# Half of the last gate chunk computed behind the first query, and first gathers in other places, in a two-layer hybrid encoder with an expert layer

## The chip, the cores and the metric
One core of a Trainium2 chip. The metric is device time in microseconds, lower is better. Everything is float32. TensorE is "PE", VectorE "DVE", ScalarE "ACT", GpSimd "POOL", SyncE "SP" in the profile.

## The reference, cut to what matters
256 tokens of 1024 features go through two layers. In each:

```
h = rmsnorm(x); proj = h @ w_in          # q, k, v, z, xbc, dt, gate_logits (2 x 1024 columns)
a_out = rmsnorm(diff_attention(q, k, v)) @ w_att_br
m_out = rmsnorm(ssd(xbc, dt) * silu(z)) @ w_ssm_br
g_att, g_ssm = split(sigmoid(gate_logits + gate_b))
x = x + (g_att * a_out + g_ssm * m_out) @ w_out
h = rmsnorm(x); qry = h @ wq             # 8 heads x 2 halves x 128
top 16 of 128 keys for both halves, top 16 of the 256 sums, softmax -> gate
x = x + sum_k gelu(u[idx_k] . h) * gate_k * v[idx_k]      # 8 x 16 = 128 experts a token
```

and a final rmsnorm. Each token has its own experts, so u and v rows are fetched by index.

## The kernel before
Tokens lie in two blocks of 128. The kernel is one hand-written program for each engine; they meet by counting semaphores. A layer has two stretches.

**Products.** Weights come through SP's queue in chunks of 128 x 4096 (2 MB) into two ring slots (w_ring), in the order of w_stream; a chunk's load waits for the first product of the chunk before it. hT holds the normed input with features on partitions. `half(c, u, m)` makes two tiles of 128 output features from a chunk, for all 256 tokens: 2 tiles x 8 k-steps, and each float32 matmul shows as two instructions, 32 in all. The last two chunks in front of the SSM branch's output product are the gate chunks C_GSSM and C_GSSM + 1 (the second gives features 512 to 1023 of g_ssm); units ("g", 2) and ("g", 3) stand around the product of the last SSM group (L651). While the last unit runs, VectorE, ScalarE and GpSimd finish the gated y of group 7, its squares and their sum. The sum of squares gives r_bc, the norm's factor. Then L460 makes m_out, 16 k-steps, four chunks; VectorE mixes (L1428 to L1433): gateT = g_att * a_out + r_bc * g_ssm * m_out. `out_product(b, c, ks)` multiplies the mixed rows of block b by half c of w_out; `add_half`/`add_quarter` on VectorE add them to x_tok. Block one's normed x is turned on TensorE (`turn_half`, `turn_quarter`) into hT and its first query (head 0) is made (`query_tiles(0, 0, ...)`), then its scores (`key_scores(0, 0)`), from the PSUM bank of which VectorE picks the first experts (`first_eight`, `other_eight`). Behind it come block two's out products, its turns, and the other queries, some of them (LATE) one tile at a time between pairs.

**Gathers.** A layer has 2 x 128 slots (block, head, rank). A slot is one indirect DMA by GpSimd (L1814): for each of the 128 tokens one row of u and v, 8 KB, 1 MB in all. Two slots are a pair; there are 128 pairs, m = 0 to 127. Five places hold pairs: ring = [a, w, d, f, c], by the lists FIRST_PLACES and PLACES. They lie over other things: w is slot 0 of w_ring (holds the first half of w_out), c lies over wq0 (first query weights), d over out1 (second half of w_out); a and f are free. So GpSimd waits, in its own order, before pair 1 (w) for out_product(1, 0), before pair 2 (d) for out_product(1, 1), before pair 6 (c) for the queries of wq0; and for `pair_used`, the product of the pair that had the place. A pair goes: gather; VectorE `dots(m)`, two multiply-and-sum of 128 x 1024 (L1671); ScalarE `weigh`: gelu (L1083), times gate (L1088), a diagonal matrix (L1095); TensorE L790, diagonals times v rows, onto the x that waits in PSUM; then the place is free. For m < 126 the steps are by pair, for the last two pairs by row.
`route(p)` on VectorE, a generator of 21 steps, makes the experts of PARTS[p] (one or two heads) between the dots: `begun_at` says with which pair it begins, and a fixed number of steps is taken behind each pair's dots. GpSimd waits for `experts_ready` before it goes on to the next part: part 1 is pairs 8 to 15, part 2 pairs 16 to 31.
ScalarE's order at the start of the stretch is written out too: `query_out` and `scores_out` copy what TensorE made, `turned(j)` copies block two's turned x, `gate_exp(p)` makes the softmax's exponentials, and they stand between the `weigh` calls.

**The end of a layer.** Block two's sums are copied out of PSUM (L1684, L839), squared (L829), the root and its reciprocal made, x normed into xn (L1219), turned (L449), copied with the gain into hT (L851), and the first product of the next layer begins; after the last layer the final norm and the store follow.

```
                for i in range(4):
                    dve.wait_ge(mix_full.sem, mix_full.at(L, 4 + i + 1))
                    step(dve.tensor_tensor(s_tmp[:, 0:2, :], two(i), gateT[:, KD + 2 * i:KD + 2 * i + 2, :], ALU.mult))
                    g = gateT[:, 2 * i:2 * i + 2, :]
                    dve.tensor_tensor(g, g, s_tmp[:, 0:2, :], ALU.add).then_inc(mix_empty.sem, 1)
```

## Time and profile before

| | us |
|---|---|
| time, median of 3 runs | 2267.85 (2266.72 to 2267.86) |
| the profiled execution's own time | 2270.27 |
| its span, first to last instruction | 2268.5 |
| TensorE matmul busy | 1770.3 (78%) |
| VectorE busy | 1348.1 (59%) |
| ScalarE busy | 737.3 (33%) |
| GpSimd busy | 600.2 (26%) |
| moved by DMA | 706.57 MB, mean 311 GB/s |

Busy shares are means over the stretches named above, which have different limits. A matmul's busy time is modelled and overlaps the next one's, so durations of runs of matmuls are better read from the chain of waits, where pieces do not overlap. Times of rows count from the start of the span. Layer one is 0 to about 1130, layer two the rest; the first gathers are issued at 478.92 and 1604.62.

### The profile page before, as it was taken

How to read it: one execution, taken by the hardware profiler on the slowest of the kernel's cores; microseconds unless marked ns; L12 is line 12 of the kernel's file. 1: busy time of each engine (PE TensorE's matmuls, PEld its weight loads, DVE VectorE, ACT ScalarE, POOL GpSimd, SP SyncE). 2: the span in 40 equal slices, each digit the busy share in tenths (PEclk: the TensorE clock that was granted, in tenths of full speed). 3: DMA queues.
4: the chain of work that ended last, by engine and by line, in shares of the span. 5: the costliest groups of instructions: out<-in, count | busy, mean ns of one | idle time of the engine just before them, and what ended most of it. 6: DMA issues, size and time to landing. Idle time of an engine off the chain costs nothing.

```text
span 2268.5 us, 26730 instructions
## 1 busy us (share of the span) xinstructions
PE 1770.3 (78%) x10064; PEld 1091.6 (48%) x10064; DVE 1348.1 (59%) x3219; ACT 737.3 (33%) x2055; POOL 600.2 (26%) x598
## 2 busy tenths in 40 slices
PE   8999999997666655555599999999977557555555
PEld 7688888864222211111186888888633222111111
DVE  3377377168776576664424674761686766676644
...
GB/s 200 153 113 148 149 221 152 287 274 421 421 421 421 421 421 421 422 422 420 375 150 119 144 123 185 193 153 284 323 420 421 421 421 421 421 422 421 422 420 294
DMA packets 91474, 706.57 MB, mean 311 GB/s; under 512 B 10800, under 2 KB 10928, under 8 KB 16848
## 3 DMA queue, kind: packets, MB, share of 16 engines
...
q14 instruction: 51, 0.42, 0.0%
...
## 4 chain that ended last, share of the span: by engine, by line
PE 50%; DMA 34%; DVE 8%; ACT 3%; POOL 2%; issue 2%; SPq 0%; POOLq 0%; DVEq 0%; ACTq 0%
PE bank L477 25%; DMA ring_c<-in_peer_uv,ex_i 13%; DMA ring_d<-in_peer_uv,ex_i 11%; DMA w_ring<-in_peer_uv,ex_i 7%; PE bank L790 6%; PE bank L460 5%; DMA ring_a<-in_peer_uv,ex_i 3%; PE bank L609 2%; PE bank L498 2%; DVE ring_c L1671 2%; PE bank L671 2%; PE bank L724 2%; DVE ring_d L1671 2%; DVE w_ring L1671 1%; ACT diag L1095 1%
## 5 line engine op out<-in xcount | busy, mean ns | idle before, releaser
L477 PE MATMUL bank<-hT,w_ring 128*128 128x256 f32 x2560 | 566.2, 381 | 0.2 <-DMA w_ring<-in_w_stream 0.2
L477 PEld LDWEIGHTS bank<-hT,w_ring 128*128 128x128 f32 x2560 | 484.0, 191 | 71.3 <-issue 6.6
L1083 ACT ACTIVATE gel<-act_u 128x2 f32<-128x2 f32 x260 | 52.8, 203 | 814.7 <-DVE ring_d L1671 173.3
L790 PE MATMUL bank<-ring_a,diag 64*64 64x512 f32 x832 | 137.9, 792 | 97.4 <-ACT diag L1095 97.4
L790 PE MATMUL bank<-ring_d,diag 64*64 64x512 f32 x832 | 134.5, 772 | 98.4 <-ACT diag L1095 98.1
L790 PE MATMUL bank<-w_ring,diag 64*64 64x512 f32 x832 | 135.0, 777 | 96.5 <-ACT diag L1095 96.5
L790 PE MATMUL bank<-ring_f,diag 64*64 64x512 f32 x800 | 131.9, 788 | 93.5 <-ACT diag L1095 93.3
L790 PE MATMUL bank<-ring_c,diag 64*64 64x512 f32 x800 | 128.0, 766 | 90.0 <-ACT diag L1095 90.0
L1814 POOL DMA_INDIRECT ring_a<-in_peer_uv,ex_i x104 | 108.4, 1043 | 306.9 <-DVE ex_i L1591 163.2
L1671 DVE SCALAR_TENSOR_TENSOR ring_a<-ring_a,h 128x1024 f32<-128x1024 f32 x104 | 123.3, 1223 | 87.4 <-DMA ring_a<-in_peer_uv,ex_i 87.2
L1671 DVE SCALAR_TENSOR_TENSOR ring_d<-ring_d,h 128x1024 f32<-128x1024 f32 x104 | 123.5, 1224 | 85.6 <-DMA ring_d<-in_peer_uv,ex_i 85.4
L1671 DVE SCALAR_TENSOR_TENSOR w_ring<-w_ring,h 128x1024 f32<-128x1024 f32 x104 | 123.3, 1222 | 81.0 <-DMA w_ring<-in_peer_uv,ex_i 80.9
L1671 DVE SCALAR_TENSOR_TENSOR ring_c<-ring_c,h 128x1024 f32<-128x1024 f32 x100 | 118.7, 1223 | 83.7 <-DMA ring_c<-in_peer_uv,ex_i 83.3
L1671 DVE SCALAR_TENSOR_TENSOR ring_f<-ring_f,h 128x1024 f32<-128x1024 f32 x100 | 118.6, 1224 | 81.5 <-DMA ring_f<-in_peer_uv,ex_i 81.4
L1095 ACT ACTIVATE diag<-cst,wgt 128x64 f32<-128x64 f32 x512 | 150.6, 340 | 8.5
L1814 POOL DMA_INDIRECT ring_d<-in_peer_uv,ex_i x104 | 110.6, 1063 | 150.5 <-PE bank L790 124.8
L1814 POOL DMA_INDIRECT w_ring<-in_peer_uv,ex_i x104 | 106.7, 1026 | 149.4 <-PE bank L790 132.6
L1814 POOL DMA_INDIRECT ring_c<-in_peer_uv,ex_i x100 | 105.3, 1053 | 148.6 <-PE bank L790 127.7
L1814 POOL DMA_INDIRECT ring_f<-in_peer_uv,ex_i x100 | 103.7, 1037 | 144.5 <-PE bank L790 128.0
L1088 ACT ACTIVATE wgt<-gel,gate_w 128x1 f32<-128x1 f32 x512 | 123.4, 287 | 9.6
L790 PEld LDWEIGHTS bank<-ring_a,diag 64*64 64x64 f32 x832 | 32.9, 163 | 194.3 <-ACT diag L1095 151.2
L790 PEld LDWEIGHTS bank<-w_ring,diag 64*64 64x64 f32 x832 | 32.2, 160 | 187.6 <-ACT diag L1095 145.7
...
## 6 DMA issues: line engine op xcount, KB each, us to landing
w_ring<-in_w_stream SPq DMA_DIRECT2D x60, 2048.0 KB, 8.3
...
wq<-in_w_stream SPq DMA_DIRECT2D x6, 2048.0 KB, 12.7
out<-in_w_stream SPq DMA_DIRECT2D x2, 2048.0 KB, 14.9
...
```

Source lines behind the costliest of these rows:

```text
L460: ins = pe.matmul(two(b0 + j // 2)[:, j % 2, :], w[:, k, j * P:(j + 1) * P], rhs(k), start=(k == 0), stop=(k == ks - 1))
L477: ins = pe.matmul(two(m % 2)[:, j % 2, :], w[:, k, j * P:(j + 1) * P], hT[:, k, :], start=(k == 0), stop=(k == KD - 1))
L498: ins = pe.matmul(bank[m % 2][:], hT[:, k, b * P:(b + 1) * P], w[:, k, :], start=(k == 0), stop=(k == KD - 1))
L609: ins = pe.matmul(two(2 + i % 2)[:, j, :], w[:, k, col:col + P], attT[:, k, :], start=(k == 0), stop=(k == KD - 1))
L671: ins = pe.matmul(bank[4 + 2 * b + c][:], gateT[:, k, b * P:(b + 1) * P], w[:, k, :], start=(k == 0), stop=(k == KD - 1))
L724: ins = pe.matmul(to[:, j * P:(j + 1) * P], w[:, k, col:col + P], hT[:, k, b * P:(b + 1) * P], start=(k == 0), stop=(k == KD - 1))
L790: ins = pe.matmul(bank[b0 + half_of][n * HB:(n + 1) * HB, :], diag[tokens, PAIR * (m % 2) + s, :], ring[PLACE[m]][tokens, s, DM + n * 512: ...
L1083: act.activation(gel[:, b, c0:c1], act_u[:, b, c0:c1], ACT.Gelu).then_inc(gelu_done.sem, 1)
L1088: ins = act.activation(wgt[:, b, j + s:j + s + 1], gel[:, b, j + s:j + s + 1], ACT.Copy, scale=gates[:, j + s:j + s + 1])
L1095: ins = act.activation(diag[:, PAIR * (m % 2) + s, :], const("blocks"), ACT.Copy, scale=wgt[:, b, j + s:j + s + 1])
L1671: ins = dve.scalar_tensor_tensor(out=row, in0=row, scalar=1.0, in1=h2[:, b, :], op0=ALU.mult, op1=ALU.mult, accum_out=act_u[:, b, PAIR * k ...
L1814: pool.indirect_dma_start(ring[q][:, s, :], None, peer_uv, bass.IndirectOffsetOnAxis(ap=ex_i[:, b, j:j + 1], axis=0))\
```

## The change
- **Gate chunk.** C_GSSM + 1 is multiplied with block one's 128 tokens only. A second load of the same chunk, gate_w1 (over ring place a), is issued by SP behind wq0, and `late_gate` makes block two's 4 tiles of 128 x 128 from it, three of its 32 matmuls before the first key scores, the others behind them. ScalarE takes the sigmoid into sc's slot 1. 
- **Mixed rows.** Block one's mixed rows stay in gateT, block two's go to a tensor of their own, mixT. For its features 512 to 1023 VectorE keeps g_att * a_out in mixT and r_bc * m_out in qryT, and `mix_late` puts them together with the late gate; out_product(1, 0) waits for this before k = 4. r_bc lies elsewhere.
- **Order.** query_tiles(2, 0) and turn_half(1, 1) move behind pair 0, and the queries and scores that follow each move one pair later, as do the first LATE tiles, the routes of parts 1 and 2 (begun with pairs 2 and 9) and ScalarE's copies; seven route steps a pair instead of six; gate_exp(0) before turned(0); softmax(0) before dots(0).
- **Places.** The first eight pairs go round f, a, w, d; place c comes in with pair 12. GpSimd waits for the late gate before pair 1, for out_product(1, 0) before pair 2, for out_product(1, 1) before pair 3.
- **Last row.** The last slot of a layer is gathered as two DMAs, its u half and its v half, with indices of their own; the dots wait for the first, TensorE for the second. Its diagonal is made from the gate ahead, and scaled by gelu.
- **Layer change.** Squares of block two, xn and the copies into hT are divided between ScalarE and VectorE; the exponential of alog comes behind them.

```diff
-M_QK, M_V, M_XBC, M_GATT, M_ATT, M_Z, M_GSSM, M_NORM2, FILLS = 4, 12, 16, 32, 36, 40, 48, 52, 75
...
-ROUTE_FILLS = [("t", 0, 0), ("t", 1, 0), ("t", 2, 0), ("q", 0, 0), ("s", 0, 0), ("t", 0, 1), ("q", 2, 0), ("t", 1, 1), ("s", 2, 0),
+M_QK, M_V, M_XBC, M_GATT, M_ATT, M_Z, M_GSSM, M_NORM2, FILLS = 4, 12, 16, 32, 36, 40, 48, 52, 76
...
+ROUTE_FILLS = [("t", 0, 0), ("t", 1, 0), ("t", 2, 0), ("q", 0, 0), ("s", 0, 0), ("g", 0, 1), ("t", 0, 1), ("q", 2, 0), ("t", 1, 1), ("s", 2, 0),
...
-LATE = [(4, 0, (1, 2, 3, 4)), (8, 0, (5, 7, 9, 11)), (12, 0, (15, 17, 19, 21)), (4, 1, (24, 26, 28, 30)),
+LATE = [(4, 0, (3, 4, 5, 6)), (8, 0, (5, 7, 9, 11)), (12, 0, (15, 17, 19, 21)), (4, 1, (24, 26, 28, 30)),
...
-FIRST_PLACES, PLACES = (0, 1, 2, 3), (0, 1, 4, 2, 3)
+FIRST_PLACES, PLACES = (3, 0, 1, 2, 3, 0, 1, 2), (3, 0, 1, 2, 4)
...
-PLACE = [FIRST_PLACES[m] if m < 4 else PLACES[(m - 4) % RING_PAIRS] for m in range(LAYER_PAIRS)]
+ALONE = len(FIRST_PLACES)
+PLACE = [FIRST_PLACES[m] if m < ALONE else PLACES[(m - ALONE) % RING_PAIRS] for m in range(LAYER_PAIRS)]
...
-        pair_a, at = place(at, "ring_a", [P, PAIR, 2 * DM])
+        pair_a, _ = place(at, "ring_a", [P, PAIR, 2 * DM])
+        gate_w1, at = place(at, "gate_w1", [P, 4096])
...
+                        sync.wait_ge(ysq_used.sem, ysq_used.at(L, 1))
+                        sync.dma_start(gate_w1[:], w_stream[CHUNKS * L + C_GSSM + 1]).then_inc(late_gate_loaded.sem, 16)
...
+                    cols = slice(0, P if c == C_GSSM + 1 else SEQ)
...
+                            ins = pe.matmul(two(m % 2)[:, j % 2, cols], w[:, k, j * P:(j + 1) * P], hT[:, k, cols],
...
-                        ins = pe.matmul(bank[4 + 2 * b + c][:], gateT[:, k, b * P:(b + 1) * P], w[:, k, :],
+                        if b == 1 and c == 0 and k == 4:
+                            wait(late_mixed, 1, L)
+                        ins = pe.matmul(bank[4 + 2 * b + c][:], mixT[:, k, :] if b == 1 else gateT[:, k, 0:P], w[:, k, :],
...
+                def late_gate(j, ks):
+                    f = FILL["g", 0, 1]
+                    to = route_bank(f) if j == 0 and ks[0] == 0 else bank[f % 4]
+                    w = gate_w1[:].rearrange("p (k n) -> p k n", k=KD)
+                    for k in ks:
+                        ins = pe.matmul(to[:, j * P:(j + 1) * P], w[:, k, j * P:(j + 1) * P], hT[:, k, P:SEQ],
+                                        start=(k == 0), stop=(k == KD - 1))
+                    if j == 3:
+                        ins.then_inc(bank_full.sem, 1)
                 def wq(c):
                     return (wq0[:], w_ring[:, ring_slot(C_OUT + 1), :], wq2[:], wq3[:])[c]
@@ -759,15 +791,17 @@
                 query_tiles(0, 0, range(2), range(4, 6))
                 wait(bank_empty, FILL["t", 2, 0] + 1, L)
                 query_tiles(0, 0, range(2), range(6, 8))
-                out_product(1, 0, range(1))
+                pe.wait_ge(late_gate_loaded.sem, late_gate_loaded.at(L, 16))
+                late_gate(0, range(3))
                 pe.wait_ge(peer_loaded.sem, peer_loaded.at(L, 32))
                 key_scores(0, 0)
-                out_product(1, 0, range(1, 8))
+                late_gate(0, range(3, 8))
+                for j in range(1, 4):
+                    late_gate(j, range(8))
+                out_product(1, 0, range(8))
                 out_product(1, 1, range(5))
                 turn_half(1, 0)
                 out_product(1, 1, range(5, 8))
-                query_tiles(2, 0, range(2))
-                turn_half(1, 1)
...
                             pe.wait_ge(diag_ready.sem, diag_ready.at(L, n_step))
+                            if n_step == LAYER_STEPS:
+                                wait(last_v, 16, L)
...
                         if m == 0:
+                            query_tiles(2, 0, range(2))
+                            turn_half(1, 1)
+                        if m == 1:
                             key_scores(2, 0)
                             wait(bank_empty, FILL["t", 1, 1] + 1, L)
                             query_tiles(0, 1, range(2))
-                        if m == 1:
+                        if m == 2:
                             query_tiles(0, 1, range(2, 4))
-                        if m == 2:
+                        if m == 3:
...
+            def squares_left(L):
+                act.activation(xn[:, 1, 0:512], x_tok[:, 1, 0:512], ACT.Square, accum_out=ssq[:, 1:2])\
+                    .then_inc(sq_done.sem, 1)
+                wait(ms_ready, 1, L)
+                act.activation(rms[:, 1:2], rms[:, 1:2], ACT.Sqrt, scale=1.0 / DM).then_inc(rms_ready.sem, 1)
...
-                    squares(0, L, 1, TB)
+                    squares_left(L)
+                    wait(rstd_known, 1, L)
+                    act.activation(xn[:, 1, 512:DM], x_tok[:, 1, 512:DM], ACT.Copy, scale=rstd[:, 1:2])\
+                        .then_inc(xn_right.sem, 1)
...
+                        c0, c1 = j + slots[0], j + slots[-1] + 1
+                        if n_step == LAYER_STEPS:
+                            last = diag[:, 2 * PAIR - 1, :]
+                            act.wait_ge(pair_used.sem, pair_used.at(L, m - 1))
+                            act.activation(last, const("blocks"), ACT.Copy, scale=gates[:, SLOTS - 1:SLOTS])\
+                                .then_inc(wgt_ready.sem, 1)
+                            act.wait_ge(dots_done.sem, dots_done.at(L, n_step))
+                            act.activation(gel[:, b, c0:c1], act_u[:, b, c0:c1], ACT.Gelu).then_inc(gelu_done.sem, 1)
+                            act.wait_ge(wgt_ready.sem, wgt_ready.at(L, n_step))
+                            act.wait_ge(gelu_done.sem, gelu_done.at(L, n_step))
+                            act.activation(last, last, ACT.Copy, scale=gel[:, b, c0:c1]).then_inc(diag_ready.sem, 1)
+                            break
...
+                act.activation(warm[:], const("ones")[:, 0:1], ACT.Sigmoid)
+                f = FILL["g", 0, 1]
+                wait(bank_full, f + 1, L)
+                for j in range(4):
+                    ins = act.activation(sc[:, 1, j, :], bank[f % 4][:, j * P:(j + 1) * P], ACT.Sigmoid,
...
+                    ins.then_inc(bank_empty.sem, 1)
+                gate_exp(0)
...
-                gate_exp(0)
                 for p, (b, h0, nh) in enumerate(PARTS):
...
+                dve.scalar_tensor_tensor(out=xn[:, 1, 512:DM], in0=x_tok[:, 1, 512:DM], scalar=1.0, in1=x_tok[:, 1, 512:DM],
+                                         op0=ALU.mult, op1=ALU.mult, accum_out=ssq_right[:]).then_inc(x_squared, 1)
+                dve.wait_ge(x_squared, 1 + L)
+                wait(sq_done, 1, L)
+                dve.tensor_scalar(rms[:, 1:2], ssq[:, 1:2], ssq_right[:], DM * EPS, ALU.add, ALU.add)\
+                    .then_inc(ms_ready.sem, 1)
...
+                for j in (1, 3):
+                    wait(bank_full, j + 1, L)
+                    cols = slice(0 if L == 0 else P, SEQ)
+                    for k in (2 * j, 2 * j + 1):
+                        ins = dve.tensor_scalar(hT[:, k, cols], two(j)[:, k % 2, cols], param("n1g", k, 1), None, ALU.mult)
+                    ins.then_inc(hT_odd.sem, 1)
...
+                dve.tensor_copy(mixT[:, 4:KD, :], gateT[:, 4:KD, right])
+                dve.tensor_tensor(gateT[:, KD + 4:2 * KD, left], gateT[:, KD + 4:2 * KD, left], bc(r_bc[:, left], 1, 4), ALU.mult)
+                step(dve.tensor_tensor(gateT[:, KD:KD + 4, :], gateT[:, KD:KD + 4, :], bc(r_bc[:], 1, 4), ALU.mult))
...
+                    cols = slice(0, SEQ if i < 2 else P)
+                    step(dve.tensor_tensor(s_tmp[:, 0:2, cols], two(i)[:, :, cols], gateT[:, KD + 2 * i:KD + 2 * i + 2, cols],
+                                           ALU.mult))
+                    if i < 2:
+                        dve.tensor_tensor(mixT[:, pair, :], gateT[:, pair, right], s_tmp[:, 0:2, right], ALU.add)
+                    else:
+                        dve.tensor_tensor(qryT[:, 1, 2 * i - 4:2 * i - 2, :], two(i)[:, :, right], bc(r_bc[:, right], 1, 2), ALU.mult)
+                    dve.tensor_tensor(gateT[:, pair, left], gateT[:, pair, left], s_tmp[:, 0:2, left], ALU.add)\
+                        .then_inc(mix_empty.sem, 1)
...
+                def mix_late():
+                    wait(bank_empty, FILL["g", 0, 1] + 1, L)
+                    step(dve.tensor_tensor(sc[:, 1], sc[:, 1], qryT[:, 1], ALU.mult))
+                    dve.tensor_tensor(mixT[:, 4:KD, :], mixT[:, 4:KD, :], sc[:, 1], ALU.add).then_inc(late_mixed.sem, 1)
...
+                    if p == len(PARTS) - 1:
+                        step(dve.tensor_scalar(last_f[:], selv[:, 0, n - 1:n], param("row0"), 2.0, ALU.add, ALU.mult))
+                        dve.tensor_copy(last_i[:, 0:1], last_f[:])
+                        step(dve.tensor_scalar(last_i[:, 1:2], last_f[:], 1.0, None, ALU.add))
...
+                mix_late()
+                next(others)
+                softmax(0)
+                dots(0)
                 add_half(1, 0)
-                next(others)
-                dots(0)
                 add_half(1, 1)
-                softmax(0)
...
-                begun_at = {1: 1, 7: 2, 14: 3, 28: 4, 44: 5, 60: 6, 76: 7, 92: 8}
+                begun_at = {2: 1, 9: 2, 14: 3, 28: 4, 44: 5, 60: 6, 76: 7, 92: 8}
...
-                        if m > 0:
-                            for _ in range(6 if m < 4 else 5 if m < 13 else 2):
+                        if m > 1:
+                            for _ in range(7 if m < 5 else 5 if m < 14 else 2):
...
                         if m == 1:
+                            pool.wait_ge(bank_full.sem, bank_full.at(L, FILL["g", 0, 1] + 1))
+                        if m == 2:
                             pool.wait_ge(mix_full.sem, mix_full.at(L, 12))
-                        if m == 2:
+                        if m == 3:
                             pool.wait_ge(mix_full.sem, mix_full.at(L, 13))
-                        if m == 6:
+                        if m == ALONE + 4:
...
+                            if j == SLOTS - 1 and b == 1:
+                                halves = peer_uv.rearrange("r (c n) -> (r c) n", c=2)
+                                pool.indirect_dma_start(ring[q][:, s, 0:DM], None, halves,
+                                                        bass.IndirectOffsetOnAxis(ap=last_i[:, 0:1], axis=0))\
+                                    .then_inc(tail_row[tail_index(m, s)].sem, 16)
+                                pool.indirect_dma_start(ring[q][:, s, DM:2 * DM], None, halves,
+                                                        bass.IndirectOffsetOnAxis(ap=last_i[:, 1:2], axis=0))\
+                                    .then_inc(last_v.sem, 16)
+                                continue
```

## Rows read from the trace of the kernel before

**Rows 1.** The page, 40 equal slices of the span: GB/s that the DMA engines moved.
```profile
GB/s 200 153 113 148 149 221 152 287 274 421 421 421 421 421 421 421 422 422 420 375 150 119 144 123 185 193 153 284 323 420 421 421 421 421 421 422 421 422 420 294
```

**Rows 2.** The chain that ended last, 380 to 500: start us, us, what, instructions.
```profile
384.68 7.11 PE bank L477 x32
...
393.68 7.10 PE bank L477 x32
...
401.76 55.49 PE bank L460 x256
...
476.79 10.30 PE bank L671 x24
...
490.10 3.57 PE bank L724 x32
...
495.13 1.72 PE bank L790 x16
```

**Rows 3.** The timeline, VectorE and GpSimd, 380 to 420: start us, us, engine, operation.
```profile
386.92 1.23 DVE L1383 TENSOR_TENSOR m_mat<-m_mat,cbm 128x1024 f32<-128x1024 f32 x1
...
396.07 1.27 POOL L1773 TENSOR_TENSOR xbc<-xbc 128x512 f32<-128x512 f32 x1 [1.54 <-ACT xbc L1009]
...
416.65 0.69 DVE L1433 TENSOR_TENSOR gateT<-gateT,s_tmp 128x512 f32<-128x512 f32 x1
```

**Rows 4.** The page, DMA issues: count, KB each, median us to landing.
```profile
w_ring<-in_w_stream SPq DMA_DIRECT2D x60, 2048.0 KB, 8.3
```

**Rows 5.** The timeline, GpSimd, 470 to 560: issues of gathers; in brackets idle before, releaser.
```profile
478.92 1.01 POOL L1814 DMA_INDIRECT ring_a<-in_peer_uv,ex_i  x1 [81.58 <-DVE ex_i L1591]
...
483.07 1.15 POOL L1814 DMA_INDIRECT w_ring<-in_peer_uv,ex_i  x1 [0.47 <-PE bank L671]
...
490.38 0.94 POOL L1814 DMA_INDIRECT ring_d<-in_peer_uv,ex_i  x1 [4.92 <-PE bank L671]
...
497.65 0.94 POOL L1814 DMA_INDIRECT ring_a<-in_peer_uv,ex_i  x1 [1.72 <-PE bank L790]
```

**Rows 6.** The timeline, VectorE, 470 to 560: dots of pairs 0, 1, 5, 7; last route step.
```profile
487.35 1.23 DVE L1671 SCALAR_TENSOR_TENSOR ring_a<-ring_a,h 128x1024 f32<-128x1024 f32 x1 [0.73 <-DMA ring_a<-in_peer_uv,ex_i]
...
493.89 1.23 DVE L1671 SCALAR_TENSOR_TENSOR w_ring<-w_ring,h 128x1024 f32<-128x1024 f32 x1 [1.32 <-DMA w_ring<-in_peer_uv,ex_i]
...
515.98 1.23 DVE L1671 SCALAR_TENSOR_TENSOR w_ring<-w_ring,h 128x1024 f32<-128x1024 f32 x1 [1.70 <-DMA w_ring<-in_peer_uv,ex_i]
...
525.92 1.23 DVE L1671 SCALAR_TENSOR_TENSOR ring_d<-ring_d,h 128x1024 f32<-128x1024 f32 x1 [2.11 <-DMA ring_d<-in_peer_uv,ex_i]
...
552.48 0.26 DVE L1572 TENSOR_SCALAR ex_i<-selv,par_all 128x32 uint32<-128x32 f32 x1
```

**Rows 7.** The timeline, ScalarE, 470 to 560.
```profile
487.56 1.14 ACT L1039 ACTIVATE hT<-bank,par_all 128x128 f32<-128x128 f32 x4 [9.10 <-PE bank L698]
...
497.81 0.20 ACT L1083 ACTIVATE gel<-act_u 128x2 f32<-128x2 f32 x1
...
498.55 0.59 ACT L1095 ACTIVATE diag<-cst,wgt 128x64 f32<-128x64 f32 x2
...
506.74 0.60 ACT L1052 ACTIVATE qryT<-bank 128x512 f32<-128x512 f32 x1 [7.61 <-PE bank L724]
```

**Rows 8.** The timeline, all engines, 1120 to 1140, where the first layer ends.
```profile
1128.12 1.09 PE L790 MATMUL bank<-ring_d,diag 64*64 64x512 f32 x8 [1.39 <-ACT diag L1095]
...
1128.36 1.23 DVE L1671 SCALAR_TENSOR_TENSOR ring_d<-ring_d,h 128x1024 f32<-128x1024 f32 x1 [1.23 <-DMA ring_d<-in_peer_uv,ex_i]
...
1129.86 0.29 ACT L1088 ACTIVATE wgt<-gel,gate_w 128x1 f32<-128x1 f32 x1
...
1130.59 1.76 PE L790 MATMUL bank<-ring_d,diag 64*64 64x512 f32 x8 [1.38 <-ACT diag L1095]
...
1133.88 1.06 ACT L829 ACTIVATE xn<-x_tok 128x1024 f32<-128x1024 f32 x1 [0.29 <-DVE x_tok L1684]
...
1135.78 0.75 DVE L1219 TENSOR_SCALAR xn<-x_tok,rstd 128x1024 f32<-128x1024 f32 x1
```

75 lines of the change are left out of this document (50 added, 25 removed).

## The prediction

> **What bounds the kernel now.** I read the page's slices first [rows 1]: each of the two layers is a stretch that moves 113 to 323 GB/s, then one at 421: the gathers of expert rows. A layer gathers 256 rows of 128 x 8 KB, 1.05 MB each, 2.49 us at 421 GB/s and 4.98 a pair; VectorE's dots of pairs 5 and 7 start 9.94 apart, both after a wait for the DMA [rows 6]. Then the chain of waits: it lies on TensorE up to the first gathers without a gap [rows 2], and after that it goes round through gathers and their products. So a layer's time is TensorE's work up to the first gather, plus 637 us of gathers, plus every microsecond in which the gather engines lack work, plus the tail after the last row. I read the change by these four; the timelines of GpSimd, VectorE and ScalarE give the hand-overs [rows 5 to 7].
>
> **Ahead of the first gather.** The last gate chunk is 64 instructions of 256 columns, 2 x 7.0 us (7.10 for 32 [rows 2], 55.49/256 x 32 = 6.94). With 128 columns I take 3.57 for 32, the row of the query tiles, also 128 columns wide [rows 2]: 6.7 us less. Of the moved half six instructions (0.67) stand ahead of the first scores, in place of two of 512 columns (0.86, from 10.30 for 24 [rows 2]): 0.2 less. Together 6.9 a layer.
> What was hidden behind that chunk: the group-7 product waits for m_mat, ready at 386.92 + 1.23 = 388.15 [rows 3]; TensorE comes there at 384.68 + 3.57 = 388.25 [rows 2]. The sum of squares ends on GpSimd at 396.07 + 1.27 = 397.34 [rows 3], 3.66 after that product's end, which is the start of the next piece of the chain, 393.68 [rows 2]; the half gate unit behind it now takes 3.57. Both are level, so I take nothing and keep 0.5 a layer as their other bound. VectorE's split mixing has three operations of 256 elements on the last unit where two of 512 stood, and out_product works on the first six tiles meanwhile. The second load of the chunk is 2 MB in SP's queue behind wq0, 5 us; its wait on ysq_used is over by then. Behind it stands the chunk for C_SSM+3: a chunk lands 8.3 us after its issue [rows 4] and is needed a whole chunk (13.9, a quarter of 55.49) later, so 5 more fit. Nothing.
>
> **The first gathers.** The clock of before is used, from the end of the first scores at 476.8. Before, pair 1 could go at 483.07, pair 2 at 490.38, pair 3 straight behind it, pair 4 at 497.65 when pair 0 was used [rows 5]. After, only the f place is free at once. TensorE does: 58 instructions of the late gate, 6.5; out_product(1,0), 16 instructions, 6.9; out_product(1,1) with one turn, 7.3; the residual and pair 0, 3.1 with a short wait for its diagonals. That is pair 1 at 483.6, pair 2 at 490.5, pair 3 at 497.9, pair 4 at 501. The late mixing hides: ScalarE's four sigmoids (1.14 as the four copies [rows 7]) and two 512-element VectorE operations (0.69 each by the mixing's own [rows 3]) take 2.6 after the late gate, and out_product needs them after 3.4.
> Then two waits appear that before had not. The query tiles (3.6) and a turn (0.4) come behind pair 0; ScalarE must copy the turned half (1.14) before it weighs pair 1 (497.81 to 499.14, 1.33 [rows 7]), and TensorE's next item is pair 1: 2.6 idle. Behind pair 2 stand query tiles alone; ScalarE copies them (0.60 [rows 7]) and weighs pair 3: 2.0 idle, where before a late query tile lay between. So, with 1.72 a pair [rows 2]: pair 1 used at 508.9, key scores and tiles 4.1, pair 2 at 514.8, tiles 3.6, wait 2.0, pair 3 at 522.0. Pair 7 needs pair 3's place and goes out at 522.3.
> From issue to dots an empty queue gave 8.4 (478.92 to 487.35 [rows 5, 6]), so pair 7 is there at 530.7. Before: 525.9 [rows 6]. 4.8 lost. Lower bound 0: without the two waits it goes at 517.4 and is there at 525.8.
> A shallow queue is slower than 4.97 a pair: from pair 1 (493.89) to pair 5 (515.98) 22.1 us for four pairs, 2.2 too many [rows 6]. Pairs 8 to 10 find such a queue again; before, it was full by then. I take 0.7, between 0 and 2.2.
> The experts of pair 16: part 2's route begins with pair 9 instead of 7 and is as long, 525.92 to 552.74 = 26.8 [rows 6]. It was early before. Now pair 16 can go at pair 9's landing + 27.1; to follow pair 15 without a gap (landing + 29.8, with 8.4 - 5.0 of lead) it had to go at + 26.4. 0.7 lost, 0 to 2.
> Sum of the start: -6.9 + 4.8 + 0.7 + 0.7 = -0.7 a layer, -1.4 in all.
>
> **The tails.** The dots of the last row wait 1.23 for it [rows 8]. As two gathers its u half is there 1.24 earlier, so the dots begin with no wait. ScalarE then needs gel and diag, not wgt between (0.33 from the 1129.86 row [rows 8]); the gate's diagonal is made while it waited. TensorE could start 1.47 earlier, at 1129.12; its product of the row before ends at 1128.12 + 1.09 = 1129.21 [rows 8], so 1.4 a layer. The v half comes when the row did. On the rows' side, queued rows follow each other at 2.49 with no fixed cost between them.
> The Trainium skill, "DMA: Bandwidth & Descriptors", section "Anatomy of one DMA — SWDGE (gpsimd) path", prices one gpsimd DMA at about 2.0 us plus its bytes at 436 GB/s, which speaks against cutting a row; were the 2.0 paid in line, the v half would come 2 later and 1.4 would shrink to nothing or less. By the pace of dots of rows 6 it isn't paid between queued rows; no run here yet shows it for halves.
> Squares by halves: 1.06 on ScalarE [rows 8] become about 0.6, the 512-element copy of rows 7, VectorE's half is beside it: 0.4 a layer. At the layer change xn is halved too, 0.75 to 0.4 [rows 8]: 0.35 once. Copies of hT on two engines: the first tile of queries waits for all transposes anyhow, nothing. In the first layer the start hangs on the first chunk's load, nothing.
> Sum: 2 x 1.4 + 2 x 0.4 + 0.35 = 3.9.
>
> **The sum.** -1.4 - 3.9 = -5.3. The profiled execution had 2270.27 (span 2268.5 and 1.8 around it); 2265.0 by that. The median of before is 2.4 under it, 2267.85, so 2262.5 for the runs.
>
> **Rivals.**
> 1. The gathers stay fed. The two waits aren't there or the queue carries over them, for which speaks that pairs 2 and 3 are issued long before they're used, against it that places, not issues, decide. Then 2 x 6.9 + 3.9 = 17.7 less: 2250; with one wait in force about 2255.
> 2. The start eats the tails: shallow queue 2.2, experts 2, both waits, 0.5 in front: 9.5 lost against 6.9, 2 x 2.6 - 3.9 = +1.3: 2269. For it speaks the 22.1 [rows 6]; against it that a refill by then is from several free places.
> 3. The split row gives nothing (the page's 2.0, or the v half): -5.3 + 2.8 = -2.5: 2265.4. Against it the pace of the rows.
> 4. Slower: VectorE holds the first dots. It sits in front of route(1) until the scores of (2,0) come at 509.7, with pairs 2 and 3 landed, then does seven route steps (3 to 4 us) between dots. I have pair 3's dots done at 516, ScalarE free for them at 518.8. From 2.8 more on this engine decides; each microsecond beyond delays pairs 7 and 16, so two layers. Slower by 0.2% wants about 5 beyond the sum in each layer, 2273. Against it the 2.8 of slack.
>
> **How the numbers follow.** Chances: forecast 0.45 (its own range 2259 to 2266), rival 1 0.20, rival 2 0.15, rival 3 0.10, rival 4 0.10. A measurement here tells about 0.2%, 4.5 us: faster is under 2263.3, slower over 2272.4. Of the forecast six tenths are under it; with rival 1 that is 0.48; the rest of it with rivals 2 and 3 is 0.42; rival 4 is 0.10. Range 2253 to 2270: it cuts off half of rival 1 and rival 4.
>
> **What would show it.** Right: the first gather 6.9 earlier after TensorE's start of the layer; GpSimd waiting on TensorE's products for pairs 3 to 7; ScalarE waiting on TensorE's turn (L1039's successor) just before it weighs pair 1; the 1 us slices of GB/s with holes up to pair 7; a last dots without a DMA wait. Wrong: pair 7 issued less than 41 us after the first gather (I have 43.5), the DMA full throughout, or a last product that waits for the v half.

## The result, and the profile after

| | before | after |
|---|---|---|
| time, median of 17 runs each | 2268.02 (2266.72 to 2270.07) | 2272.2 (2268.1 to 2276.7) |
| ratio to before | | 1.0017, 95% interval 1.0011 to 1.0024 |
| the profiled execution's own time | 2270.27 | 2271.85 |
| its span | 2268.5 | 2270.0 |

The forecast was 2262.5 and a range of 2253 to 2270. Instead of 5.3 us faster, the change made the kernel 3.9 us slower by the ratio (4.2 by the medians). That is within the 0.2% that the prediction called no change. The 17 times of the changed kernel lie 8.6 us apart, those of the kernel before 3.4; no run here shows why. One of the six runs of the kernel start, further on, took 6826.82 us and is left out of its numbers.

**The start of the layer.** The chain that ended last, kernel after, 380 to 520: start us, us, what, instructions.

```profile
384.35 3.77 PE bank L496 x32
...
395.06 55.25 PE bank L476 x256
...
469.85 6.48 PE bank L738 x58
476.32 11.16 PE bank L692 x26
...
498.05 1.14 ACT hT L1089 x4
...
499.83 0.59 ACT diag L1156 x2
...
500.47 1.95 PE bank L826 x16
...
512.31 0.60 ACT qryT L1102
...
514.19 1.95 PE bank L826 x16
```

(L477, L460 and L790 of the kernel before are L496, L476 and L826 here.) L496 is a half gate unit, 3.77 where a whole one took 7.10 [rows 2]; m_out begins at 395.06 in place of 401.76 [rows 2]. L738 is the late gate, L692 the out products. The two waits that the prediction named are both there: ScalarE's copy of the turned half stands in front of pair 1's weights, its copy of query (0,1) in front of pair 3's, and TensorE waits for each:

The timeline, TensorE, kernel after, 490 to 520: the products of pairs 1 and 3; in brackets idle before, releaser.

```profile
500.47 1.95 PE L826 MATMUL bank<-ring_a,diag 64*64 64x512 f32 x16 [2.45 <-ACT diag L1156]
...
514.19 1.95 PE L826 MATMUL bank<-ring_d,diag 64*64 64x512 f32 x16 [1.91 <-ACT diag L1156]
```

**The gathers.** The timeline, GpSimd, kernel after, 471 to 568: first rows of pairs 0, 2, 3, 5, 7 and 16.

```profile
471.98 1.02 POOL L1941 DMA_INDIRECT ring_f<-in_peer_uv,ex_i  x1 [78.10 <-DVE ex_i L1707]
...
483.47 0.94 POOL L1941 DMA_INDIRECT w_ring<-in_peer_uv,ex_i  x1 [4.39 <-PE bank L692]
...
490.77 0.94 POOL L1941 DMA_INDIRECT ring_d<-in_peer_uv,ex_i  x1 [5.12 <-PE bank L692]
...
502.72 0.94 POOL L1941 DMA_INDIRECT ring_a<-in_peer_uv,ex_i  x1 [4.85 <-PE bank L826]
...
516.44 1.03 POOL L1941 DMA_INDIRECT ring_d<-in_peer_uv,ex_i  x1 [4.70 <-PE bank L826]
...
565.49 1.68 POOL L1941 DMA_INDIRECT ring_d<-in_peer_uv,ex_i  x1 [8.83 <-DVE ex_i L1688]
```

The first gather goes out at 471.98, 6.94 before the 478.92 of [rows 5]; 6.9 was forecast. Of the 6.94, 0.33 had been there when TensorE came to the gate chunk (384.35 against 384.68 [rows 2]), so the chunk gave 6.6. But from pair 3 on, GpSimd waits for products, and at pair 16 for 8.83 us for experts. The timeline, VectorE, kernel after: the first dots of pairs 7, 8, 9 and 16.

```profile
527.51 1.23 DVE L1787 SCALAR_TENSOR_TENSOR ring_d<-ring_d,h 128x1024 f32<-128x1024 f32 x1 [4.04 <-DMA ring_d<-in_peer_uv,ex_i]
...
533.43 1.23 DVE L1787 SCALAR_TENSOR_TENSOR ring_f<-ring_f,h 128x1024 f32<-128x1024 f32 x1 [3.54 <-DMA ring_f<-in_peer_uv,ex_i]
...
538.42 1.22 DVE L1787 SCALAR_TENSOR_TENSOR ring_a<-ring_a,h 128x1024 f32<-128x1024 f32 x1 [2.61 <-DMA ring_a<-in_peer_uv,ex_i]
...
575.88 1.22 DVE L1787 SCALAR_TENSOR_TENSOR ring_d<-ring_d,h 128x1024 f32<-128x1024 f32 x1 [0.48 <-DMA ring_d<-in_peer_uv,ex_i]
```

Dots of pair 7 start at 527.51, 55.5 after the first gather, where [rows 6] had 47.0. Busy time by windows, kernel after: window, length, busy PE, PEld, DVE, ACT, POOL, clock granted to TensorE, DMA share, GB/s.

```profile
514.00:518.00 4.00, 3.81 (x33) 2.45 (x34) 3.79 (x10) 0.84 (x4) 1.26 (x2) 1.00 0.72 281
518.00:522.00 4.00, 3.88 (x34) 2.32 (x33) 3.95 (x7) 3.07 (x10) 1.64 (x2) 1.00 0.97 315
522.00:526.00 4.00, 4.00 (x36) 2.52 (x35) 0.81 (x5) 3.40 (x8) 2.80 (x3) 1.00 0.93 344
526.00:530.00 4.00, 4.00 (x41) 3.03 (x39) 2.38 (x4) 0.08 (x1) 1.13 (x2) 1.00 0.95 354
530.00:534.00 4.00, 4.00 (x40) 2.38 (x32) 0.57 (x1) 1.79 (x6) 1.88 (x2) 1.00 1.01 418
...
566.00:570.00 4.00, 3.14 (x16) 0.62 (x16) 2.88 (x12) 3.94 (x7) 3.09 (x4) 0.64 0.59 182
```

The pace of 421 is reached only at 530, 58 us after the first gather, and is lost once more in front of pair 16. Beside the first layer of before, in us from each kernel's first gather ("landed" is the second row's issue plus the time to landing that the DMA view gives for it):

| pair | issued, before | after | landed, before | after |
|---|---|---|---|---|
| 1 | 4.15 | 4.62 | 14.9 | 15.2 |
| 3 | 13.94 | 18.79 | 27.1 | 28.8 |
| 5 | 24.32 | 30.74 | 37.1 | 41.3 |
| 7 | 31.95 | 44.46 | 47.0 | 55.5 |
| 9 | 40.75 | 53.27 | 56.9 | 66.4 |
| 16 | 79.52 | 93.51 | 92.2 | 103.9 |

Pair 3 is 1.7 late, pair 7 8.5, pair 9 9.5, pair 16 11.7. Dots of row 254, the last but one, start 646.97 after the first gather before and 658.38 after: 11.4 lost in layer one. The second layer lost 7.6 (649.86 and 657.45). Up to pair 24 it is 12.6 and 8.9; 1.2 to 1.3 of this is made up again by row 254, and no run here shows by what.

**The tail.** The timeline, all engines, kernel after, 1129 to 1138, which answers to [rows 8]:

```profile
1130.36 1.22 DVE L1787 SCALAR_TENSOR_TENSOR ring_c<-ring_c,h 128x1024 f32<-128x1024 f32 x1 [1.26 <-DMA ring_c<-in_peer_uv,ex_i]
...
1131.62 1.23 DVE L1787 SCALAR_TENSOR_TENSOR ring_c<-ring_c,h 128x1024 f32<-128x1024 f32 x1
...
1133.19 0.35 ACT L1141 ACTIVATE diag<-diag,gel 128x64 f32<-128x64 f32 x1
...
1133.59 0.21 PEld L826 LDWEIGHTS bank<-ring_c,diag 64*64 64x64 f32 x8 [0.79 <-ACT diag L1141]
...
1136.29 0.63 ACT L868 ACTIVATE xn<-x_tok 128x512 f32<-128x512 f32 x1
```

The last row's dots follow those of row 254 without a wait for the DMA, gelu stands alone in front of its diagonal, TensorE waits for that and not for the v half, and the squares are 0.63 instead of 1.06. From the dots of row 254 to the next layer's first product it is 10.51 after and 12.47 before; to the store at the end 8.75 and 10.59. The 1.96 at the layer change isn't the tails' alone. The last product before took 1.76 there [rows 8], with a granted clock of 0.59 from 1130.5 to 1132.5, and 1.09 at the end of layer two (granted clock 1.00 from 2259 to 2260.5), which is 0.67 in the changed kernel's favour; and TensorE then waits 0.45 for the next layer's first chunk, which it didn't before. Without the two it is 1.7, where 2.15 was forecast (1.4 + 0.4 + 0.35); at the end of layer two it is 1.84 for 1.8.

The sum of these readings: layer one -6.94 + 11.41 - 1.96 = +2.5; layer two, from its first product, -6.35 + 7.59 - 1.84 = -0.6; together 1.9 longer, and the spans differ by 1.5 (the store itself ended 0.4 sooner). The profiled execution of before was 2.3 above the median of its 17 runs and that of after 0.35 under its own, so the medians differ by 4.2 and these two traces by 1.6.

### The profile page after: what moved, and what is told of

Its sections match the earlier page's. It is cut to its first block, busy times and chain, and to the rows that moved or that the text cites. A ratio compares the mean times of both kernels' runs of the same rounds, so it can differ in the third digit from the quotient of the medians.

```text
span 2270.0 us, 27041 instructions
## 1 busy us (share of the span) xinstructions
PE 1781.2 (78%) x10192; PEld 1098.8 (48%) x10192; DVE 1352.3 (60%) x3253; ACT 739.0 (33%) x2060; POOL 613.0 (27%) x600
## 3 DMA queue, kind: packets, MB, share of 16 engines
q8 instruction: 80, 1.31, 0.2%
## 4 chain that ended last, share of the span: by engine, by line
PE 50%; DMA 34%; DVE 7%; ACT 4%; POOL 3%; issue 2%; SPq 0%; POOLq 0%; ACTq 0%; DVEq 0%
PE bank L496 24%; DMA w_ring<-in_peer_uv,ex_i 17%; DMA ring_d<-in_peer_uv,ex_i 12%; PE bank L826 7%; PE bank L476 5%; DMA ring_a<-in_peer_uv,ex_i 4%; DVE w_ring L1787 3%; PE bank L628 2%; PE bank L517 2%; DVE ring_d L1787 2%; PE bank L756 2%; PE bank L692 2%; ACT diag L1156 1%; PE bank L670 1%; POOL w_ring L1941 1%
## 5 line engine op out<-in xcount | busy, mean ns | idle before, releaser
L496 PE MATMUL bank<-hT,w_ring 128*128 128x256 f32 (+1 forms) x2560 | 552.9, 376 | 0.7 <-DMA w_ring<-in_w_stream 0.7
L496 PEld LDWEIGHTS bank<-hT,w_ring 128*128 128x128 f32 x2560 | 474.4, 191 | 69.0 <-issue 6.6
L1144 ACT ACTIVATE gel<-act_u 128x2 f32<-128x2 f32 (+1 forms) x258 | 52.4, 203 | 810.5 <-DVE ring_c L1787 167.9
L826 PE MATMUL bank<-ring_a,diag 64*64 64x512 f32 x832 | 142.8, 817 | 109.9 <-ACT diag L1156 109.9
L826 PE MATMUL bank<-w_ring,diag 64*64 64x512 f32 x832 | 140.3, 804 | 91.8 <-ACT diag L1156 91.8
L826 PE MATMUL bank<-ring_d,diag 64*64 64x512 f32 x832 | 136.8, 785 | 86.3 <-ACT diag L1156 86.3
L826 PE MATMUL bank<-ring_f,diag 64*64 64x512 f32 x832 | 132.6, 764 | 91.3 <-ACT diag L1156 91.0
L1941 POOL DMA_INDIRECT ring_f<-in_peer_uv,ex_i x104 | 113.4, 1091 | 289.4 <-DVE ex_i L1707 156.2
L826 PE MATMUL bank<-ring_c,diag 64*64 64x512 f32 x768 | 120.8, 754 | 87.5 <-ACT diag L1156 87.5
L1787 DVE SCALAR_TENSOR_TENSOR ring_f<-ring_f,h 128x1024 f32<-128x1024 f32 x104 | 123.4, 1224 | 82.5 <-DMA ring_f<-in_peer_uv,ex_i 82.5
L1787 DVE SCALAR_TENSOR_TENSOR ring_c<-ring_c,h 128x1024 f32<-128x1024 f32 x96 | 114.0, 1223 | 77.4 <-DMA ring_c<-in_peer_uv,ex_i 77.1
L1941 POOL DMA_INDIRECT ring_c<-in_peer_uv,ex_i x94 | 99.9, 1062 | 124.4 <-PE bank L826 109.2
L826 PEld LDWEIGHTS bank<-ring_a,diag 64*64 64x64 f32 x832 | 33.0, 164 | 206.5 <-ACT diag L1156 163.1
L826 PEld LDWEIGHTS bank<-w_ring,diag 64*64 64x64 f32 x832 | 32.9, 164 | 189.8 <-ACT diag L1156 146.7
## 6 DMA issues: line engine op xcount, KB each, us to landing
out<-in_w_stream SPq DMA_DIRECT2D x2, 2048.0 KB, 16.2
```

The lines of the kernel that those rows point to most:

```text
L496: ins = pe.matmul(two(m % 2)[:, j % 2, cols], w[:, k, j * P:(j + 1) * P], hT[:, k, cols], start=(k == 0), stop=(k == KD - 1))
L826: ins = pe.matmul(bank[b0 + half_of][n * HB:(n + 1) * HB, :], diag[tokens, PAIR * (m % 2) + s, :], ring[PLACE[m]][tokens, s, DM + n * 512: ...
L1144: act.activation(gel[:, b, c0:c1], act_u[:, b, c0:c1], ACT.Gelu).then_inc(gelu_done.sem, 1)
L1787: ins = dve.scalar_tensor_tensor(out=row, in0=row, scalar=1.0, in1=h2[:, b, :], op0=ALU.mult, op1=ALU.mult, accum_out=act_u[:, b, PAIR * k ...
L1941: pool.indirect_dma_start(ring[q][:, s, :], None, peer_uv, bass.IndirectOffsetOnAxis(ap=ex_i[:, b, j:j + 1], axis=0))\
```

## The experiments

The kernel before had medians of 2267.87, 2268.36 and 2267.80 beside the three sets. "lag" is how much later the dots of pair 24 start, counted from the first gather, than in the kernel before (131.93) in layer one.

| kernel | median us | ratio to before, 95% interval | lag |
|---|---|---|---|
| after | 2272.2 | 1.0017 (1.0011 to 1.0024) | 12.6 |
| tails | 2264.19 | 0.9985 (0.9977 to 0.9994) | -0.5 |
| lastrow | 2265.85 | 0.9988 (0.9979 to 0.9997) | -0.3 |
| start | 2275.97 | 1.0036 (1.0023 to 1.0049) | 10.6 |
| actorder | 2263.69 | 0.9981 (0.9972 to 0.9991) | 8.1 |
| cseven | 2265.53 | 0.9992 (0.9983 to 1.0) | 9.5 |
| route7 | 2268.74 | 1.0002 (0.9993 to 1.0011) | 10.2 |
| combo | 2255.96 | 0.9943 (0.9929 to 0.9956) | 4.4 |
| oldorder | 2265.62 | 0.9986 (0.9977 to 0.9995) | 8.2 |
| oldseven | 2264.87 | 0.9987 (0.9978 to 0.9996) | 6.4 |
| r1late | 2256.22 | 0.9946 (0.9932 to 0.9959) | 2.9 |
| four | 2275.61 | 1.0028 (1.0018 to 1.0038) | 4.1 |
| together | 2270.12 | 1.0011 (1.0002 to 1.002) | -2.2 |

### The change cut in two: tails, lastrow and start

tails is the kernel before with the last row in two DMAs, divided squares, xn and copies. lastrow has the split row and its diagonal alone. start is the changed kernel with neither.

```diff
+                            if j == SLOTS - 1 and b == 1:
+                                halves = peer_uv.rearrange("r (c n) -> (r c) n", c=2)
+                                pool.indirect_dma_start(ring[q][:, s, 0:DM], None, halves,
+                                                        bass.IndirectOffsetOnAxis(ap=last_i[:, 0:1], axis=0))\
+                                    .then_inc(tail_row[tail_index(m, s)].sem, 16)
+                                pool.indirect_dma_start(ring[q][:, s, DM:2 * DM], None, halves,
+                                                        bass.IndirectOffsetOnAxis(ap=last_i[:, 1:2], axis=0))\
+                                    .then_inc(last_v.sem, 16)
```

> The kernel before with the tails alone: last row as two DMAs, squares, normed x and hT copies divided. My theory (the tails gave what was forecast, 1.9 at each layer end, and the start of the gathers lost about 4 a layer net): 3.8 under the kernel before, some 2264.2. Rival (the tails only look shorter in the changed kernel because its gathers end in another rhythm): within 1 of the kernel before, 2267 to 2268. The split row giving nothing: about 1 under.

> The changed kernel without the tails: half gate chunk, late gate, order and places alone. My theory: 8 over the kernel before (4.2 measured for the whole change plus 3.8 of tails), some 2276. Rival (tails worth nothing): some 2272.

> The kernel before with only the last row of a layer as two DMAs and its diagonal made ahead; squares, xn and hT copies as before. The prediction gave this 2 x 1.4 of the tails' 3.9. My theory: 2.5 to 2.8 under the kernel before, some 2265. Rival (the halves of squares and xn carry most): within 1.5 of the kernel before.

tails 2264.19 against 2264.2 expected, start 2275.97 against 2276. The two halves of the change add up (-3.7 and +8.1 to +4.4, and the whole measured 4.2), so the tails are worth about what was forecast (3.9; the ratio gives 3.4, between 1.4 and 5.2) and the miss is in the start, which was to give 1.4 and cost 8.1. lastrow gave 2.0 by the medians and 2.7 by the ratio (0.7 to 4.8), against 2.8 forecast: the split row gives something, its size to half a microsecond isn't resolved.

### The two waits: actorder

```diff
-                        if m == 0:
+                        if m == 1:
                             query_out(2, 0)
                             turned(1)
-                        if m == 1:
                             scores_out(2, 0)
-                        if m == 2:
-                            query_out(0, 1)
                         if m == 3:
+                            query_out(0, 1)
                             scores_out(0, 1)
```

> The changed kernel with ScalarE weighing pair 1 ahead of the copies of query (2,0) and of the turned half, and pair 3 ahead of the copies of query (0,1), so that TensorE has pair 1's and pair 3's diagonals when it comes to them. My theory (each microsecond on the chain of products up to pair 3 holds up the gathers of pairs 5 to 7 and, by the route, pair 16): waits of 2.45 and 1.91 go, pair 7 is issued about 4 earlier than 44.5 after the first gather, 4 a layer, 8 in all, some 2264. Rival (the gathers are slow for themselves when few are queued, the products don't matter): pair 7's dots no earlier than 54, within 2 of the changed kernel. Rival (VectorE's route steps hold the first dots): the wait moves from ScalarE's copies to the dots, about 1 to 2 a layer gained.

2263.69, 8.5 under the changed kernel. Pair 7 is issued at 39.94 instead of 44.46 and its dots start at 50.62 instead of 55.5; both waits of TensorE are gone. The chain that ended last, this kernel, 465 to 570:

```profile
497.84 1.88 PE bank L826 x16
...
500.39 0.39 ACT sc L1113
500.81 0.50 DVE vals L1599 x2
...
504.70 2.27 DVE ring_d L1785 x4
...
509.94 2.29 DVE ring_f L1785 x4
...
514.88 2.29 DVE ring_a L1785 x4
```

Pair 1's product (497.84) now follows the turn at once. The first rival, that the products don't matter, wanted dots of pair 7 no earlier than 54; it is out. What is late next is VectorE: it takes the scores of query (2,0) at 500.81 and seven route steps before the dots of pair 3 (ring_d, 504.70), which had landed at 500.84 (the second row's issue at 491.84 plus 9.0). This is rival 4's place; it carries the chain only with the two waits gone.

### The places: cseven and four

```diff
-FIRST_PLACES, PLACES = (3, 0, 1, 2, 3, 0, 1, 2), (3, 0, 1, 2, 4)
+FIRST_PLACES, PLACES = (3, 0, 1, 2), (3, 0, 1, 4, 2)
...
-                        if m == ALONE + 4:
+                        if m == ALONE + 3:
```

> The changed kernel with place c taken into the round from pair 7 on instead of pair 12 (four alone, then f, a, w, c, d). My theory: pair 7 no longer waits for pair 3's product and is issued 4 to 5 earlier, pair 8 about 4 earlier, five places from there on; the lag of pair 9 behind the kernel before falls from 9.5 to about 5, so 8 in all, some 2264. Rival (not the places but the slow issue to landing of 10.4 to 11, whatever is queued): the pairs land no earlier, within 2 of the changed kernel.

2265.53, 6.7 under the changed kernel where 8 were expected, with both waits still in it (2.45 and 1.91 again). Pair 7 now waits only for the queries that use wq0, and goes out at 42.12, 2.3 earlier where 4 to 5 were expected. The timeline, GpSimd, this kernel:

```profile
515.74 0.94 POOL L1941 DMA_INDIRECT ring_c<-in_peer_uv,ex_i  x1 [0.82 <-PE bank L756]
```

four is the kernel before with `PLACES = (0, 1, 2, 3)`, four places to the end.

> The kernel before with four places instead of five for all pairs (a, w, d, f; c never). Measures what a shorter queue costs by itself. A pair in an empty queue took 10.5 to 10.8 from its first issue to its landing in both kernels, one behind another pair about 12; a place comes back about 6 after its landing. My theory (the gather engines lose pace only while fewer than about two pairs are queued): four places keep 2 to 3 pairs queued, so 0.1 to 0.3 a pair is lost at most, 2270 to 2300. Rival (any shortening of the queue costs pace in proportion): 0.5 a pair or more, over 2390.

2275.61, 7.2 over the kernel before, over 256 rows. From 600 us on it moved 421 GB/s as before did; between 560 and 600 it was 398. Pair 24 is 4.1 late in layer one and 3.4 in layer two, which is about all of the 7.2; in layer one it was 0.5 at pair 7 and 3.7 at pair 17, and in between GpSimd waited for products alone. So four places are enough to keep the engines full once the queue is full; they cost in the stretch in which it has to be filled, and there the changed kernel too has only four, up to pair 11.

### The experts of pair 16: route7

```diff
-                            for _ in range(7 if m < 5 else 5 if m < 14 else 2):
+                            for _ in range(7 if m < 12 else 2):
```

> The changed kernel with seven route steps a pair instead of five for pairs 5 to 11, so that the experts of pair 16 (part 2, route begun with pair 9) are made behind three pairs and not five. My theory: GpSimd's wait of 8.83 for them before pair 16 falls by the two pairs' dots, some 4.6, less what VectorE's longer stretches hold up; 3 a layer, some 2266. Rival (the hole at pair 16 costs nothing beyond the lag already there, because the places are late as well): within 1 of the changed kernel, 2271 to 2273.

2268.74: 3.5 gained where 6 were expected. The wait for experts before pair 16 is gone, and another stands in its place. The timeline, GpSimd, this kernel:

```profile
562.60 1.16 POOL L1941 DMA_INDIRECT ring_d<-in_peer_uv,ex_i  x1 [4.51 <-PE bank L826]
```

Pair 16 goes out 2.8 earlier (90.73), held by the product of the pair that had its place, pair 11: with seven steps behind each dots VectorE comes to that pair at 82.4 instead of 80.3.

### All three: combo and r1late

combo has the edits of actorder, cseven and route7.

> The changed kernel with three edits at once: ScalarE weighs pairs 1 and 3 before its copies, place c joins from pair 7 on, and seven route steps a pair through pair 11. Apart, the first gave 8.5 and the second 6.7 against the changed kernel's 2272.2. My theory (all three act on when places and experts of the first 17 pairs come free, and partly save the same microseconds): 12 to 14 under the changed kernel, 2258 to 2260, below both kernels and below the tails alone. Rival (they save the same microseconds entirely, since VectorE, which holds dots of pair 3 by 3.8 in the first of them, is next): 2262 to 2264.

2255.96, 16.2 under the changed kernel, more than expected, and 12.4 under the kernel before (0.57% by the ratio). It is the fastest one here. Apart the three gave 8.5 + 6.7 + 3.5 = 18.7, each to about 2, so they hardly save the same microseconds. Pair 7 goes out at 38.05 and pair 16 at 84.29. At row 254 of layer one it is only 2.3 behind the kernel before (649.28 from the first gather). Its first gather goes out at 473.79, 5.1 ahead of before and not 6.9, because TensorE's very first products end 1.8 later than in the changed kernel's trace; of the 5.1 in front 2.8 stays in layer one. The three edits were not run on a kernel without the half chunk, so how much of the 12.4 is owed to the earlier gather isn't shown.

r1late is combo with `0 if m < 3 else 11 if m < 5` in front of the 7, which puts the dots of pair 3 ahead of the route of part 1.

> The kernel with the three edits (2255.96) and with VectorE's route of part 1 begun behind the dots of pair 3 instead of pair 2 (11 and 10 steps behind pairs 3 and 4), so that VectorE no longer stands at the scores of query (2,0) with pair 3 landed (there its dots began 3.8 late). My theory (VectorE is next in line for pair 3, but pairs 8 and 9 wait for pair 3 and 4 alone): 0 to 1.5 a layer, 2253 to 2256. Rival (11 steps in one stretch hold up pair 4 by as much): no change or 1 to 2 slower.

2256.22: no change. The dots of pair 3 start at 29.21, as soon as it has landed, instead of 32.83; but those of pair 5 at 43.33 instead of 43.02, and pair 8 goes out at 43.69 instead of 43.38. So the dots of pair 3 were not what pairs 8 and 9 waited for: GpSimd stands in front of pair 8 for the experts of part 1 in both (2.11 in combo, 3.06 here).

### The order of the kernel before: oldorder and oldseven

oldorder is the changed kernel with query (2,0) and the turn ahead of pair 0 again:

```diff
                 out_product(1, 1, range(5, 8))
+                query_tiles(2, 0, range(2))
+                turn_half(1, 1)
...
-                begun_at = {2: 1, 9: 2, 14: 3, 28: 4, 44: 5, 60: 6, 76: 7, 92: 8}
+                begun_at = {1: 1, 7: 2, 14: 3, 28: 4, 44: 5, 60: 6, 76: 7, 92: 8}
```

and all that follows a pair earlier; oldseven has cseven's places too.

> The changed kernel with the order of the kernel before: query (2,0) and block two's second turn ahead of pair 0, queries, scores, first late tiles and routes of parts 1 and 2 a pair (two for part 2) earlier, six route steps. Half chunk, late gate, places and tails stay. My theory: pair 0 is used 4.0 later, the waits of 2.45 and 1.91 are gone, so pair 7 goes out as before it (44 after the first gather), but part 2's experts come about two pairs earlier and pair 16 goes out near 90 instead of 93.5: 3 a layer, some 2266. Rival (only what stands ahead of pair 0 counts): 4 a layer slower, some 2280.

> The changed kernel with the order of the kernel before and place c from pair 7 on. My theory: order alone gave 2265.6; pair 7 no longer waits for pair 3's product and goes out 2 to 3 earlier than 44.2; pairs 8 and 9 follow. 1 to 2 a layer, 2262 to 2264. Rival (part 1's experts or VectorE's dots are level with it): within 1 of 2265.6.

oldorder 2265.62, as expected: pair 7 goes out at 44.24, no earlier than in the changed kernel, but pair 16 at 84.99 instead of 93.51. So of the changed kernel's parts the new order by itself made it 6.6 slower. oldseven 2264.87: here the rival holds. Pair 7 is 1.2 earlier and pair 16 goes out at 84.99 again; place c is worth 6.7 with the new order and 0.8 with the old, which the runs can't tell from nothing.

### What a pair costs in an empty queue: together

```diff
-                            if m == 0 and s == 1:
+                            if m == 0 and s == 0:
                                 wait(first_experts, 1, L)
```

> The kernel before with GpSimd holding the very first gather until the second's experts are there too, so that the two rows of pair 0 are issued some 1.25 apart and not 2.73. It measures what a pair costs in an empty queue. My theory (rows queued together share the engines: pair 1 took 10.8 from its first issue to its dots, and pair 0 with its 8.4 did so only because its second row came 2.7 later): dots of pair 0 at 10.3 to 10.8 after the first issue, rows landing after some 8 and 9.3. Rival (8.4 is what a pair costs from its first issue, as the prediction took it): 8.4, or less. The time stays within 2 of the kernel before, since TensorE comes to pair 0 only 16 after the first issue.

Neither number held. The DMA view of this kernel, windows around the first row's issue and around the second's, 1.31 later: median us to landing.

```profile
ring_a<-in_peer_uv,ex_i POOLq DMA_INDIRECT x1, 5.5
...
ring_a<-in_peer_uv,ex_i POOLq DMA_INDIRECT x1, 7.8
```

The timeline, VectorE, this kernel, the first dots:

```profile
491.20 1.22 DVE L1671 SCALAR_TENSOR_TENSOR ring_a<-ring_a,h 128x1024 f32<-128x1024 f32 x1 [4.90 <-DMA ring_a<-in_peer_uv,ex_i]
```

The first gather was at 481.94, so dots came 9.26 after it. A pair whose rows go out together into an idle queue takes 9.1 to 9.3; the 8.4 of [rows 5, 6] was a pair whose rows went out 2.73 apart and landed 5.7 and 5.6 after their issues, as one row does with nothing else under way (5.5). The 10.8 of pair 1 (483.07 to 493.89 in the same rows) and the 11.1 of the changed kernel's pair 7 were pairs issued while the rows of the pair before were still on their way. The time was 2.3 over before, just outside the 2 expected; all of layer one's gathers began 3.0 later (481.94 against 478.92) and pair 24 had made up 2.2 of it.

## Why the prediction was wrong, by its own steps

**Ahead of the first gather, -6.9.** Nearly right: 6.6 in layer one without the 0.33 that lay ahead of the gate chunk, 6.35 in layer two, counted from the layer's first product. The cover behind the half chunk nearly held: the sum of squares lies on the chain, its product starts at 393.93 straight behind GpSimd, and the half unit would have been done about 0.3 earlier (390.04 + 3.57). Nothing was taken for it, with 0.5 as the other bound.

**The tails, -3.9.** Right: 3.7 by tails (1.4 to 5.2 by its ratio).

**The two waits, 2.6 and 2.0.** Right in place and size (2.45 and 1.91), and pair 7 was issued 44.5 after the first gather where the prediction had 43.5. actorder shows what they cost: 8.5 in the two layers.

**From issue to dots, 8.4: the step that failed.** "From issue to dots an empty queue gave 8.4 ..., so pair 7 is there at 530.7." The kernels after and start have the same program up to the tail, so their four layers are four readings of this step. The timeline, VectorE, the first dots of pair 7 in layer two of after and in both layers of start:

```profile
1654.71 1.22 DVE L1787 SCALAR_TENSOR_TENSOR ring_d<-ring_d,h 128x1024 f32<-128x1024 f32 x1 [2.43 <-DMA ring_d<-in_peer_uv,ex_i]
...
525.81 1.22 DVE L1724 SCALAR_TENSOR_TENSOR ring_d<-ring_d,h 128x1024 f32<-128x1024 f32 x1 [2.58 <-DMA ring_d<-in_peer_uv,ex_i]
...
1655.07 1.23 DVE L1724 SCALAR_TENSOR_TENSOR ring_d<-ring_d,h 128x1024 f32<-128x1024 f32 x1 [2.19 <-DMA ring_d<-in_peer_uv,ex_i]
```

| pair 7, from the first gather | issued | dots | from issue to dots | later than before |
|---|---|---|---|---|
| after, layer one | 44.46 | 55.53 | 11.1 | 8.5 |
| after, layer two | 44.45 | 53.93 | 9.5 | 7.1 |
| start, layer one | 44.45 | 54.07 | 9.6 | 7.1 |
| start, layer two | 45.96 | 55.19 | 9.2 | 8.4 |
| mean | 44.83 | 54.68 | 9.85 | 7.8 |

It took 9.2 to 11.1, never 8.4. The prediction read the price of a pair from the only pair whose rows were issued far apart, and called the queue of pair 7 empty when pair 6's rows were still in it (in layer one of after they landed 45.0 and 47.9 after the first gather, pair 7 was issued at 44.5). Pair 1, in the same rows, had 10.8. Of the 2.7 by which the 11.1 is over 8.4, together shows 0.7 to 0.9 to be the rows' distance; that the rest is pair 6's rows on their way is read from the landings, and no run took them away. Pair 7 was 3.0 later than forecast (7.8 for 4.8): about half of this is the price, and nearly as much its issue, 44.8 in the mean for 43.5: three products took 1.95, 1.88 and 1.95 where 1.72 was taken, and small pieces beside them were longer too.

**The experts of pair 16, 0.7.** Its mechanism was right: the wait is there, and in all four layers pair 16 went out at pair 9's landing plus 27.1. The same price was wrong in it: with 10.4 from issue to dots, as in layer one of after, it should have gone out by + 24.4 and not + 26.4, and 2.7 are lost. Measured, from pair 9 to pair 17: 3.1 and 1.3 in the two layers of after, 2.7 and 1.5 in those of start. oldorder and route7 show that this can be had back.

**The shallow queue, 0.7.** 1.0 from pair 7 to pair 9 in layer one of after, 0.4 in layer two.

With layer one's 10.8 for 8.4 at pair 7 and 10.4 at pair 16 the start reads -6.9 + 7.3 + 0.7 + 2.7 = +3.8 a layer, the sum 7.6 - 3.9 = +3.7, and the forecast 2271.6, 0.6 from the median. That it comes so near is partly luck, for these are among the dearest readings. With the mean of 9.85 in both places it is -6.9 + 6.35 + 0.7 + 2.15 = +2.3 a layer, and 2268.6, which is 6.1 of the 9.7 by which the forecast missed. The 3.6 left are the later issue of pair 7 (1.3 a layer), the front (0.3 and 0.55 in the two layers), and 2.7 between traces and medians (1.6 and 4.2), less what has been made up by row 254 (1.2 and 1.3). So the mechanisms were those named, and what failed is above all one duration, used twice, which was too small by 0.8 to 2.7. The prediction's bounds had let every other term vary and this one not, which is also why the range ended at 2270. Its signs of being wrong (pair 7 issued before 41, the DMA full throughout, a last product that waits for the v half) didn't come either: they tested the path and not the price.

**The rivals.** Rival 1 (the gathers stay fed) fell: the windows show 281 to 354 GB/s up to 530. Rival 2 (the start eats the tails) came nearest: its 9.5 lost a layer is the mean of the measured 11.4 and 7.6, and its +1.3 stands against the 1.9 read above. It reached that by other terms, with the 8.4 in it as well. Rival 3 (the split row gives nothing) fell by tails; the fixed cost that the Trainium skill, "DMA: Bandwidth & Descriptors", section "Anatomy of one DMA — SWDGE (gpsimd) path", gives to every gpsimd DMA is not paid in line behind a queued row: dots of the last row start 1.26 after those of row 254, at 1131.62, so the u half had landed by then, and TensorE loads the last weights at 1133.59 with no wait for the v half, 1.97 later. With 2.0 and the transfer in line for each half it could not have been there. Rival 4 (VectorE) doesn't hold in the changed kernel, where the copies of ScalarE are later (dots of pair 3 end at 509.6, ScalarE is free for them at 512.91), and does in actorder.

**Still open.** Why layer one of after loses 11.4 up to row 254 and layer two 7.6. It isn't the layer: start, with the same program up to there, loses 8.4 in layer one and 10.1 in layer two, so one layer of one trace is good to about 2 us here, and the means (9.5 and 9.3) are what can be compared. Nor did a run here separate the pace of a few rows in flight from the delay of a row that is issued late; the table of landings shows only both together.
